# Expert gathers issued ahead of the wait for a scatter's landing, with 4096-byte weight packets, in a two-layer encoder with a routed mixture of experts

## The reference

```python
    b, s, dm = h.shape
    t = h.reshape(-1, dm)
    scores = jax.nn.sigmoid((t @ w_router).astype(jnp.float32))
    ...                                     # the best group of 4 experts, then its 2 best: expert_idx
    gate = jnp.sum(jax.nn.one_hot(expert_idx, N_EXPERTS, dtype=jnp.float32) * w[..., None], axis=1)
    out = jnp.zeros_like(t)
    for e in range(N_EXPERTS):
        a = jax.nn.silu(t @ w_gate[e]) * (t @ w_up[e])
        out = out + gate[:, e:e + 1] * (a @ w_down[e])
```

## Time and profile before

| what | value |
|---|---|
| median of 3 runs | 1626.04 us (1623.54 to 1630.99) |
| the profiled execution | 1626.85 us, its span 1625.0 us |
| TensorE busy | 1447.3 us (89%) |
| VectorE / ScalarE / GpSimd busy | 1014.8 / 873.9 / 129.2 us |
| moved by DMA | 341.46 MB, 317.20 MB of it on q1 |
| expert loop of layer 0, first to last turn of rows | 488.05 to 764.01 us |
| expert loop of layer 1, the same | 1280.98 to 1555.34 us |

### The profile page before, as it was taken

How to read it: one execution, slowest core, us unless ns; L and a number is a source line. 1 busy time by engine, 2 the same in 40 slices (tenths; PEclk the granted TensorE clock), 3 DMA queues, 4 the chain that set the end, 5 groups by cost and what they waited for, 6 DMA issues and landing times.

```text
span 1625.0 us, 19382 instructions
## 1 busy us (share of the span) xinstructions
PE 1447.3 (89%) x6822; PEld 1099.2 (68%) x6822; DVE 1014.8 (62%) x1276; ACT 873.9 (54%) x1242; POOL 129.2 (8%) x143
## 2 busy tenths in 40 slices
PE   6799989999779999999769989899995999999986
PEld 3577658887557777777537765688772777777764
DVE  1465675325577888888372938633347688888874
ACT  4532585223337677777363228822325477777764
POOL 1000000000011222211000000000000012122110
PEclk9899999999879999999889999999997899999997
DMA  9532561112249999999762137411232799999944
GB/s 330 190 105 102 207 245 62 58 52 104 104 162 335 336 355 341 346 346 348 259 236 104 52 123 247 150 52 52 103 105 104 273 345 355 354 349 339 344 171 159
DMA packets 148368, 341.46 MB, mean 210 GB/s; under 512 B 8351, under 2 KB 10545, under 8 KB 148176
## 3 DMA queue, kind: packets, MB, share of 16 engines
q1 hardware_dynamic: 136880, 317.20, 54.2%
q0 software_dynamic: 10704, 22.57, 3.8%
q10 hardware_dynamic: 720, 0.84, 0.2%
HBM read 333.05 MB, written 24.12 MB: 220 GB/s over the span
## 4 chain that ended last, share of the span: by engine, by line
PE 57%; DMA 16%; DVE 8%; issue 8%; ACT 8%; POOLq 2%; PEldq 0%; DVEq 0%; SPq 0%; ACTq 0%; PEld 0%
PE bank L735 11%; PE bank L737 11%; PE bank L736 11%; DMA y_by_choice<-zone,row_now 7%; DMA zone<-rows_by_token,row_now 6%; PE bank L1085 2%; PE bank L1087 2%; PE bank L1086 2%; PE bank L768 2%; POOLq L2317 1%; PE bank L1070 1%; PE bank L1072 1%; PE bank L1071 1%; PE bank L1034 1%; DMA ring<-in_w_in 1%
## 5 line engine op out<-in xcount | busy, mean ns | idle before, releaser
L735 PE MATMUL bank<-x_hi,w_lo 128*128 128x512 f32 x608 | 245.9, 404 | 28.3 <-DVE x_lo L1681 17.4
L737 PE MATMUL bank<-x_hi,w_hi 128*128 128x512 f32 x608 | 239.0, 393 | 0.0
L736 PE MATMUL bank<-x_lo,w_hi 128*128 128x512 f32 x608 | 238.7, 393 | 0.0
L2174 DVE TENSOR_TENSOR w_lo<-ring,x_lo 128x2048 fp32r<-128x2048 f32 x92 | 210.7, 2290 | 32.3 <-ACT x_lo L1480 29.2
L1480 ACT CAST zone_r<-ring 128x2048 fp32r<-128x2048 f32 x92 | 175.8, 1911 | 36.4 <-PE bank L1072 23.3
L1480 ACT CAST x_lo<-ring 128x2048 fp32r<-128x2048 f32 x92 | 176.0, 1918 | 27.7 <-PE bank L1087 14.6
L1658 DVE TENSOR_TENSOR w_lo<-ring,w_hi 128x1024 fp32r<-128x1024 f32 x84 | 102.4, 1221 | 98.6 <-ACT w_hi L1227 98.2
L1070 PE MATMUL bank<-w_lo,zone_r 128*128 128x512 f32 x384 | 157.8, 411 | 1.9 <-issue 1.9
L735 PEld LDWEIGHTS bank<-x_hi,w_lo 128*128 128x128 f32 x608 | 114.9, 189 | 65.3 <-issue 26.2
L736 PEld LDWEIGHTS bank<-x_lo,w_hi 128*128 128x128 f32 x608 | 115.4, 190 | 25.2 <-issue 2.4
L737 PEld LDWEIGHTS bank<-x_hi,w_hi 128*128 128x128 f32 x608 | 115.2, 190 | 25.1
(11 more groups left out here) (308 smaller groups left out, 2817.2 us busy)
## 6 DMA issues: line engine op xcount, KB each, us to landing
ring<-in_w_gate SPq DMA_DIRECT2D x32, 2048.0 KB
ring<-in_w_up SPq DMA_DIRECT2D x32, 2048.0 KB, 13.8
ring<-in_w_down SPq DMA_DIRECT2D x32, 2048.0 KB, 8.9
ring<-in_w_ada SPq DMA_DIRECT2D x24, 2048.0 KB, 8.8
ring<-in_w_in SPq DMA_DIRECT2D x16, 2048.0 KB, 8.4
ring<-in_w_out SPq DMA_DIRECT2D x4, 2048.0 KB, 8.4
zone<-y_by_choice SPq DMA_DIRECT2D x8, 1024.0 KB, 8.2
ring<-in_w_branch_a SPq DMA_DIRECT2D x2, 2048.0 KB, 7.7
```

The costliest lines, as they stand in the source:

```text
L735: mm(out, lo, x_first, start=start, stop=False)
L736: mm(out, hi, x_second, start=False, stop=False)
L737: return mm(out, hi, x_first, start=False, stop=stop)
L2174: v.tensor_tensor(w_low[EXPERT_SLOTS[par][k]][:, cols], ring[EXPERT_SLOTS[par][k]][:, cols], part_hi[buf].bitcast(F32), ALU.subtract)\
```

## The change

GpSimd's list is put in another order: the gather of tile n+3 is issued right behind the scatter of tile n, and the wait for that scatter's landing comes behind the gather. The gate and up weights are loaded with two neighbouring rows per partition, so that a packet is 4096 bytes; to match, ScalarE's copy to `rows_tok` permutes columns by reading PSUM with a stride of two elements. And VectorE's `low_part` of group 18 moves from period 7 to period 8, behind `probs_b`.

```diff
                 for k, (name, s) in enumerate(zip(("w_gate", "w_up", "w_down"), EXPERT_SLOTS[0])):
                     sp.wait_ge(used[s], layer * SLOT_BLOCKS[s] + SLOT_BLOCKS[s])
-                    sp.dma_start(ring[s][:, :].rearrange("p (k n) -> p k n", k=(KC, KC, FC)[k]),
-                                 t_in[name][layer:layer + 1, 0, :, :].rearrange("o (k p) n -> p (o k) n", p=P))\
+                    j = (2, 2, 1)[k]
+                    sp.dma_start(ring[s][:, :].rearrange("p (b n) -> p b n", b=FC),
+                                 t_in[name][layer:layer + 1, 0, :, :].rearrange("o (b p j) n -> p (o b) (j n)", p=P, j=j))\
                       .then_inc(w_landed[0][k], 16)
...
                 def load_weights(k, e, par):
                     name = ("w_gate", "w_up", "w_down")[k]
-                    sp.dma_start(ring[EXPERT_SLOTS[par][k]][:, :].rearrange("p (k n) -> p k n", k=(KC, KC, FC)[k]),
+                    j = (2, 2, 1)[k]
+                    sp.dma_start(ring[EXPERT_SLOTS[par][k]][:, :].rearrange("p (b n) -> p b n", b=FC),
                                  t_in[name][layer:layer + 1, bass.ds(e, 1), :, :]
-                                 .rearrange("o e (k p) n -> p (o e k) n", p=P))\
+                                 .rearrange("o e (b p j) n -> p (o e b) (j n)", p=P, j=j))\
                       .then_inc(w_landed[par][k], 16)
...
                         ps = wait_full(act, use, ("rows", t, half))
-                        nc.scalar.copy(rows_tok[:, t, half * 512:(half + 1) * 512], ps[:, :])\
+                        nc.scalar.copy(rows_tok[:, t, half * 512:(half + 1) * 512]
+                                       .rearrange("p (b j i) -> p b j i", b=2, j=2),
+                                       ps[:, :].rearrange("p (b i j) -> p b j i", b=2, j=2))\
                             .then_inc(S["rows_ready"], 1)
...
                     if 1 <= p <= PERIODS:
                         probs_b(p - 1)
+                    if p == PERIODS:
+                        low_part(QKV_GROUPS)
                     if p < PERIODS:
...
                     for n in GROUP_PERIOD.get(p, ()):
-                        low_part(QKV_GROUPS + n)
+                        if n > 0:
+                            low_part(QKV_GROUPS + n)
...
-                def expert(p, par, last=False):
...
+                def fetch(p, par):
+                    pool.wait_ge(xgT_done, (before + p) * 2 + par + 1)
+                    nc.gpsimd.sem_inc(passed, 1)
+                    gather(par, index_of(0, p * 2 + par + 2, par))
+                def send(p, par):
+                    pool.wait_ge(y_ready, (before + p) * 2 + par + 2)
+                    nc.gpsimd.sem_inc(passed, 1)
+                    scatter(par, index_of(1, p * 2 + par, par))
+                def sent(p, par):
+                    pool.wait_ge(y_sent[par], (before + p) * 16 + 16)
+                    nc.gpsimd.sem_inc(y_stored[par], 16)
+                fetch(0, 0)
+                send(0, 0)
+                with pool.Fori(0, rest - 1) as p:
+                    fetch(p, 1)
+                    sent(p, 0)
+                    send(p, 1)
+                    fetch(p + 1, 0)
+                    sent(p, 1)
+                    send(p + 1, 0)
+                fetch(rest - 1, 1)
+                sent(rest - 1, 0)
+                send(rest - 1, 1)
+                sent(rest - 1, 1)
+                send(rest, 0)
+                sent(rest, 0)
+                send(rest, 1)
+                sent(rest, 1)
```

More of the change, by code:

```diff
@@ L2318, in index_of @@
                     return now
-                def expert(p, par, last=False):
[L2321 to L2327, removed]
-                    nc.gpsimd.sem_inc(passed, 1)
-                    scatter(par, index_of(1, tile, par))
+                def fetch(p, par):
+                    pool.wait_ge(xgT_done, (before + p) * 2 + par + 1)
+                    nc.gpsimd.sem_inc(passed, 1)
+                    gather(par, index_of(0, p * 2 + par + 2, par))
[4 more added lines that the diff above has]
+                def sent(p, par):
                     pool.wait_ge(y_sent[par], (before + p) * 16 + 16)
                     nc.gpsimd.sem_inc(y_stored[par], 16)
[L2333 to L2337, removed]
+                fetch(0, 0)
[15 more added lines that the diff above has]
+                sent(rest, 1)
                 nc.gpsimd.drain().then_inc(arrived, 1)
```

## The result

The changed kernel takes 1619.88 us (median of 20 runs, 1610.02 to 1624.95), the kernel before 1627.83 (20 runs of the same session). The ratio is 0.9945, with a 95% interval of 0.9929 to 0.9961: 0.55% faster, barely more than what can be told from no change, and 26 us from the 1594 that was forecast. The profiled execution after has a span of 1619.5 us; before it was 1625.0.

What follows compares the result with a forecast made beforehand. It took the expert loops to be bound by TensorE's list and a nearly equal ring of scatter, gather and turn, with gathers late. 1626.85 - 27.1 (gathers) - 5.4 (`low_part`) = 1594.3, forecast 1594 us, range 1588 to 1609.

Steps and rivals of the forecast that it cites:

- The failed step: GpSimd's list in the expert loops: moving the landing wait behind the gather removes 7.63 us in front of it.
- the term of 27.1: Expert loops: gathers in time take 27.1 us off the kernel, bounds 29.1 and 14.
- the ring: Expert loops: the cycle of scatter, gather and turn, nearly as long as TensorE's list; 19.63 us a tile.
- The fifth rival: No change that can be told: the gather stays as late, attention part alone gives 1621 us; chance 0.04.
- The term that then decided: Gate and up loads: 4096-byte packets worth nothing beside the old order, up to 0.2 us a tile beside the new.
- 3.2 us or more in hand: Expert loops: the gather lands at + 11.9 to + 15.3 us, TensorE needs it at + 18.5, so the stall goes.
- TensorE's own tile of 18.51 us: Expert loops: what one tile takes on TensorE without a gather wait, small waits for VectorE included.
- The sixth rival: ScalarE's cast of gate weights: the gate load lands late in every tile, kernel slower, 1635 us; chance 0.04.
- The reserve of 1.4 us: Expert loops: time in hand for the gate load before ScalarE casts it, called thin but holding.
- the serial case: Same DMA queue: gather rows move only after the scatter lands, landing at + 18.3 us, or 1.7 us late.
- the 2.7: End of attention, layer 0: moving `low_part` saves 2.7 us, 1.3 from ScalarE's list and 1.4 from TensorE's clock.
- The strided copy: ScalarE's 8 copies reading PSUM with a stride: cost taken as 0, upper bound 2.7 us per layer.

Runs made afterwards that it cites:

- e1: The changed kernel with `index_of` waiting on a semaphore raised by the index copy instead of draining: 1602.1 us.
- e8: e1 with one drain put back at the head of `fetch`, ahead of the gather's index copy: 1632.7 us.
- e7: The changed kernel with 2048-byte packets and the plain copy, keeping the new order and the moved `low_part`: 1599.3 us.
- e3: The changed kernel with GpSimd's list of the kernel before; 4096-byte packets, strided copy and moved `low_part` stay: 1631.4 us.
- e2: The changed kernel with both index copies and one drain ahead of the wait for `y_row`, so nothing stands between scatter and gather: 1596.5 us.
- e6: e2 with 2048-byte packets: 1592.6 us.
- e9: e2 with SyncE loading the gate weights of tile n+2 ahead of the down weights of tile n+1, 4096-byte packets: 1590.5 us.
- e5: The kernel before with only the 4096-byte packets and the strided copy that goes with them: 1635.5 us.
- e4: The kernel before with only `low_part` moved, 2048-byte packets: 1624.4 us.
- e12: e9 with gate and up weights in 8192-byte packets: 1590.3 us.
- e10: e6 with SyncE loading the gate weights of tile n+2 ahead of the down weights of tile n+1, 2048-byte packets: 1593.4 us.

## Why the prediction was wrong

**The failed step: "Removed from in front of the gather: 7.63 us. What is left is the scatter's 1.02 us from + 2.67, an index copy and 0.92 us of issue."** The row that I read had its wait ahead of the index copy, and the wait instruction was moved. But `index_of` drains, and a drain waits for the scatter too (e1 against e8). Of the mean 10.55 us between the two starts 1.9 went at 2048 bytes (e7) and 1.1 at 4096 (after; 1.3 against e3, which has its packets). With short packets that was worth 25 us, close to the term of 27.1, but not by its mechanism: the gather still waited for every scatter, and the ring had only 1.1 us to lose. The prediction listed the landing's wait and the copy as what stands ahead of the gather; it priced the copy and left out the drain behind it. The row that would have told is the 5.07 us at 489.44. The fifth rival named the cause, "GpSimd's list is blocked elsewhere", with a chance of 0.04 and a time of 1621; 1619.9 was measured. That it came so near is in part luck: it had nothing from the order and nothing from the packets, where the runs show 11.5 us gained and 7 lost.

**The term that then decided: the packets at 0.** "So the packets are worth nothing beside the old order and up to 0.2 us a tile beside the new" counted what they save and not what they do to the transfers they share the engines with. They cost 7 to 9 us beside the old order and about 20 beside the new. That term was safe only with "3.2 us or more in hand", which the drain took away. Either of the two corrected alone brings the forecast back into its range of 1588 to 1609: without the drain's wait 1596.5 to 1602.1 (e2, e1), with short packets 1599.3 (e7). With both it is 1592.6 (e6).

**What was right.** TensorE's own tile of 18.51 us as the floor behind the ring: 18.56 us in e9. The 29.1 us that late gathers cost: e6 takes out 27.1 in its loops (510.4 to 483.3). The rates of a lone load, 386 and 418 GB/s: e5 has 418 at 4096. The sixth rival's place, ScalarE's cast of gate weights: it waits 22 times in e2, but for 2.7 us at most, and 5.0 us of loop are what it is worth (e9). The reserve of 1.4 us that I gave the gate load was not there.

**Small slips in the working.** From its rows the gather would start at + 4.8 to + 6.4, not + 4.9 to + 6.6; in the serial case with the long instruction it would land at + 20.0, 1.5 us late and not 1.7; and 2.82 against 1.6 us for the transposes is 1.2 us from the clock, not 1.4. None of them carries weight.

**The gather in the same queue.** In e2 the scatter of 563.97 was down at 572.5 and the gather issued at 565.63 at 574.9, by the landing events in the trace; over the 26 tiles they are 2.5 us apart. If the gather's rows had moved only after the scatter it would be near 579.5, 7.0 us later. The rule weighed in the prediction (the Trainium skill, DMA: Bandwidth & Descriptors, Queues, rings and completion order) has descriptors of one ring taken in order, but lets a later one finish its write before an earlier one, so the serial sum was the prediction's reading and not the rule. The trace doesn't show that sum, and it did not decide the case.

**`low_part`: right in kind, its size not settled.** The first turn of layer 0 came 2.8 us earlier (488.05 to 485.26), the 12 transposes 2.9, the first gate group 2.4. That the turn agrees with the 2.7 is partly chance: over the twelve profiles with the move it lies between 484.50 and 489.29 (mean 485.9), over the three without it between 487.88 and 489.53 (mean 488.5). In layer 1 of the changed kernel's profile the granted clock was 0.50 at the same place (window 1034 to 1038), but in e4's it was 1.00:

```profile
1034.00:1038.00 4.00, 2.61 (x20) 1.85 (x20) 1.35 (x2) 3.43 (x11) 0.00 (x0) 1.00 0.94 379
```

As a whole the move gave 2.7 us in e4, near the lower bound of 2.6, where 5.4 were forecast; e4's interval holds both.

**The strided copy: right at 0.** 5.47 us for 8, and the wait behind it the same.

**Where the 8 us come from.** By e3, e4 and the kernel itself: `low_part` 2.7 us faster, the packets 7.0 slower, the order 11.5 faster, 7.2 in sum; 8.0 were measured against the kernel before of its own session. These are steps along one path, so their sum is no check of its own, and the order and the packets don't simply add: with short packets the order is worth 25.

## What to carry to other kernels

Before moving an instruction past a wait, read everything that its helper emits, drains and fences above all: what they wait for is not in their line. Then measure how far the ring is from the next bound: here it was 1.1 us a tile, so 1.9 us of reordering was worth 25 us, and about 1 us of slower landings took some 20 us back. Larger packets for a bulk stream are no free change while small latency-bound transfers run beside it; price both, and try the change with and without them.

The best kernels here are e9 and e12 (both copies and one drain ahead, gate weights first): 1590.5 and 1590.3 us, 2.2 to 2.3% faster than before, and not to be told from e6 and e10. The 4096-byte packets are not what does it.

## What the hardware showed that was not expected

A drain on GpSimd waited for an indirect transfer in flight, 8.4 and 8.9 us of idle time behind a scatter in the tiles shown, and 5.07 us behind a gather; a semaphore on the copy in its place did not.

An index copy of 128x1 on GpSimd took from 0.18 to 2.35 us, both in e1, and 2.32 in the tile shown. The prediction's bound of 1.83 was too low (the trace of before has 2.30 at 598.87), which didn't matter in e1: TensorE waited for no gather in its loops.

Landings beside a bulk load depend on its packets: 7.6, 8.3 and 8.3 us for a scatter and 8.3, 9.5 and 9.9 for a gather at 2048, 4096 and 8192 bytes, while the load by itself runs at 386, 418 and 434 GB/s in the windows shown. The Trainium skill (DMA: Bandwidth & Descriptors, Why small descriptors are slow) has a fixed cost for each packet, by the estimate in the prediction 2.2% more at 2048 bytes than at 4096. 386 to 418 is 8%, so the rows show a good deal more than that from this step; 406 to 410, the nearest pair of all kernels, would be 1%.
